# Forget-gate layer: values and decays computed among the input projections, 128 tokens per score tile, one carried state, norm by pairs of heads

## The reference, cut to what matters

```
proj = h @ w_in                                   # q_pre, f_pre, i_val, g_out, 1024 columns each
f = lb + (1 - lb) * sigmoid(f_pre);  k = 1 - f;  q = silu(q_pre)
b = cumsum(log f, inside a chunk);  b_ref = b[C/2 - 1];  b_last = b[C - 1]
scores = (q * exp(b - b_ref)) @ (k * exp(b_ref - b)).T, causal, inside a chunk
o_intra = scores @ v
q_dec = q * exp(b);  k_dec = k * exp(b_last - b)
for each chunk:  o_inter = q_dec @ S;  S = exp(b_last) * S + k_dec.T @ v
o = o_intra + o_inter
o = o * rsqrt(mean(o^2 over the head) + eps) * norm_g * silu(g_out)
y = o @ w_out
```

## Time and profile before

| | us |
|---|---|
| median of 3 runs | 2901.13 |
| range | 2897.42 to 2907.69 |
| the profiled execution | 2895.93 |
| its span | 2893.8 |
| TensorE busy | 2489.5 |
| VectorE busy | 2036.6 |
| ScalarE busy | 1397.0 |

### The profile page before, as it was taken

The page is one execution under the profiler, slowest core; times in us unless marked ns, Lnnn a source line. Parts: engine busy times, 40 slices in busy tenths (PEclk is TensorE's granted clock), DMA queues, the critical chain, the costliest instruction groups (busy, mean ns, idle before and its releaser), DMA issues. The chain is left out here.

```text
span 2893.8 us, 46933 instructions
## 1 busy us (share of the span) xinstructions
PE 2489.5 (86%) x18972; PEld 2361.8 (82%) x18972; DVE 2036.6 (70%) x3448; ACT 1397.0 (48%) x2474; POOL 92.4 (3%) x85
## 2 busy tenths in 40 slices
PE   3888999988789998859999569997777999976998
PEld 3677999967789998749999469997557999865997
DVE  3476788645767875978877638886247788757885
ACT  4543565356155644436635316745314575433673
POOL 0010000000100000800000000000000000000000
PEclk8799999988899999979999759999978999988999
DMA  4022667722045776214567204573104556641452
GB/s 183 31 86 74 233 220 290 302 91 88 15 169 196 263 286 235 90 37 157 199 263 277 73 2 160 194 289 115 59 0 175 206 194 245 243 175 38 153 195 96
DMA packets 63367, 462.91 MB, mean 160 GB/s; under 512 B 7024, under 2 KB 7088, under 8 KB 7216
## 3 DMA queue, kind: packets, MB, share of 16 engines
q1 hardware_dynamic: 62640, 456.16, 42.6%
q10 hardware_dynamic: 512, 3.77, 0.3%
HBM read 458.85 MB, written 1.05 MB: 159 GB/s over the span
## 5 line engine op out<-in xcount | busy, mean ns | idle before, releaser
L727 PE MATMUL psum<-arena_rounded,upper_rounded 128*128 128x256 f32 (+1 forms) x5208 | 1477.8, 284 | 149.6 <-PEq L629 55.2
L728 PE MATMUL psum<-arena_rounded,upper_rounded 128*128 128x256 f32 (+1 forms) x5208 | 1464.7, 281 | 0.0
L729 PE MATMUL psum<-arena_rounded,ring_rounded 128*128 128x256 f32 (+1 forms) x5208 | 1464.5, 281 | 0.0
L727 PEld LDWEIGHTS psum<-arena_rounded,upper_rounded 128*128 128x128 f32 (+1 forms) x5208 | 992.4, 191 | 167.6 <-issue 87.6
L544 DVE TENSOR_TENSOR ring_rounded<-ring,upper_rounded 128x1024 fp32r<-128x1024 f32 (+4 forms) x990 | 847.2, 876 | 336.3 <-ACT upper_rounded L535 331.5
L535 ACT ACTIVATE upper_rounded<-ring 128x1024 fp32r<-128x1024 f32 (+4 forms) x990 | 758.1, 775 | 636.3 <-PE psum L729 543.9
L728 PEld LDWEIGHTS psum<-arena_rounded,upper_rounded 128*128 128x128 f32 (+1 forms) x5208 | 997.0, 191 | 1.5 <-issue 1.4
L729 PEld LDWEIGHTS psum<-arena_rounded,ring_rounded 128*128 128x128 f32 (+1 forms) x5208 | 995.0, 191 | 0.1
L566 DVE SCALAR_TENSOR_TENSOR ada_sum<-ring,small,ada_sum 128x1024 f32<-128x1024 f32 x168 | 214.7, 1278 | 1.0
L2372 DVE SCALAR_TENSOR_TENSOR arena<-psum,cols,arena 128x255 f32<-128x255 f32 (+1 forms) x352 | 153.2, 477 | 55.5 <-ACT arena L2339 52.4
L2339 ACT ACTIVATE arena<-psum,cols 128x256 f32<-128x256 f32 x176 | 89.4, 561 | 44.2 <-PE psum L729 44.2
(11 more groups left out here) (460 smaller groups left out, 2551.3 us busy)
## 6 DMA issues: line engine op xcount, KB each, us to landing
ring<-stream_dram SPq DMA_DIRECT2D x434, 1024.0 KB, 4.9
const<-const_dram ACTq DMA_DIRECT2D x1, 1607.0 KB, 7.1
x<-x_dram ACTq DMA_DIRECT2D x1, 1024.0 KB, 9.1
out_dram<-x SPq DMA_DIRECT2D x1, 1024.0 KB, 3.9
cols<-cols_dram ACTq DMA_DIRECT2D x1, 982.0 KB, 10.6
...
```

Source lines behind the costliest of these rows:

```text
L727: pe.matmul(out, upper, x[0][:, b.k, :], start=(b.k == 0), stop=False)
L728: pe.matmul(out, upper, x[1][:, b.k, :], start=False, stop=False)
L729: ins = pe.matmul(out, lower, x[0][:, b.k, :], start=False, stop=(b.k == nk - 1))
```

## The change

`hgrn_in` now opens with the feed-forward block before it and holds four projections in the order f, values, q, g, each of f and q with one side number. GpSimd writes the scan's restart marks. ScalarE takes the logarithm of f during the values, VectorE scans and subtracts during q, ScalarE takes the exponentials during g, by halves of four heads, and VectorE multiplies. The gate keeps its raw value until the next block.

`hgrn` is one block. The 256 tokens are two tiles of 128. Inside each tile, scores inside a chunk are as before (16 matmuls); scores beyond a chunk are 48 matmuls of a chunk's 32 decayed keys with all later queries of the tile, which have been multiplied by the decays of the chunks between. Both land in one 128 x 128 score tile. Only one state per head is left, that after the first 128 tokens, from 8 transposes and 8 matmuls. The output takes 3 matmuls per head. Norm, gate and split go by pairs of heads. The diff, cut (removed code is in the kernel above):

```diff
-            g["hg_qfg", i] = with_sides(by_rounds(matrix("hg_w_in_2", (0,), D, tiles(0, 2 * KD))
-                                                  + matrix("hg_w_in_2", (0,), D, tiles(3 * D, KD)), TOGETHER), sides(2))
+            part = lambda n: matrix("hg_w_in_2", (0,), D, tiles(n * D, KD))
+            g["hg_f", i] = with_sides(by_rounds(part(1), TOGETHER), sides(1))
             g["hg_v", i] = by_rounds(matrix("hg_w_in_2", (0,), D, tiles(2 * D, 2, BANK)))
+            g["hg_q", i] = with_sides(by_rounds(part(0)), sides(1))
...
+    return [slot2(chip, n) for n in (1, 2, 3, 5, 6, 7, 8, 9, 10)]
...
+    @block.gpsimd
+    def _(pool):
+        pool.memset(t2, 1.0).then_inc(restart_ready, 1)
+        pool.wait_ge(restart_ready, 1)
+        pool.memset(chunks(t2)[:, :, 0:1], 0.0).then_inc(restart_ready, 1)
+
+    def forget(block, s, banks, steps):
...
+            for c in range(steps):
+                s["act_step"](act, c)
+                act.wait_ge(s["ready"], s["through"](c))
+                if c >= 2:
+                    act.wait_ge(forgets_ready, c - 1)
+                act.activation(e[c % 2], banks(c)[0], ACT.Sigmoid).then_inc(s["free"], 1)
+            w.act(act, s["last"])
...
+            for c in range(steps):
+                s["dve_step"](dve, c)
+                dve.wait_ge(s["free"], c + 1)
+                dve.tensor_scalar(f[:, c, :], e[c % 2], chip.lb_rest[:, c:c + 1], chip.lb[:, c:c + 1],
+                                  ALU.mult, ALU.add).then_inc(forgets_ready, 1)
+                if c:
+                    dve.wait_ge(forgets_ready, c)
+                    dve.tensor_scalar(k[:, c - 1, :], f[:, c - 1, :], -1.0, 1.0, ALU.mult, ALU.add)
+            dve.wait_ge(forgets_ready, KD)
...
+    @block.tensor
+    def _(pe):
+        for at, b in enumerate(blocks):
+            n = at // KD
+            if at == KD:
+                pe.wait_ge(fs["free"], 6)
+            if at == 0 or blocks[at - 1].chunk is not b.chunk:
+                pe.wait_ge(w.lower_ready, b.chunk.order + 1)
+            upper, lower = w.parts(b)
+            for tt in range(NT):
+                bank, sl = chip.bank(v_bank(n, tt), b.width), slice(tt * P, (tt + 1) * P)
+                pe.matmul(bank, h[0][:, b.k, sl], upper, start=(b.k == 0), stop=False)
+                pe.matmul(bank, h[0][:, b.k, sl], lower, start=False, stop=False)
+                ins = pe.matmul(bank, h[1][:, b.k, sl], upper, start=False, stop=(b.k == KD - 1))
+            if b is b.chunk.end:
+                ins.then_inc(w.used, 1)
+
...
+        for n in range(2):
+            act.wait_ge(forgets_ready, KD)
+            act.activation(f[:, halves[n], :], f[:, halves[n], :], ACT.Ln).then_inc(logs_ready, 1)
+            w.act(act, ends[n] - 1)
+            act.wait_ge(w.used, ends[n] + 1)
+            act.activation(v[:, 0, n * BANK:(n + 1) * BANK], chip.bank(v_bank(n, 0)), ACT.Identity).then_inc(v_ready, 1)
+        w.act(act, ends[1])
+
+    @block.vector
+    def _(dve):
+        for n in range(2):
+            w.dve(dve, ends[n] - 1)
+            dve.wait_ge(w.used, ends[n] + 1)
+            dve.tensor_copy(v[:, 1, n * BANK:(n + 1) * BANK], chip.bank(v_bank(n, 1))).then_inc(v_ready, 1)
+        w.dve(dve, ends[1])
...
+            for c in range(steps):
+                s["dve_step"](dve, c)
+                if c == 0:
+                    dve.wait_ge(restart_ready, 2)
+                    dve.wait_ge(fs["dve_done"], 1)
+                part = halves[c // 4]
+                at = lambda n: chunks(b_sum[:, part, :])[:, :, n:n + 1].broadcast_to([P, KD // 2 * (T // C_HG), C_HG])
+                if c % 4 == 0:
+                    dve.wait_ge(logs_ready, c // 4 + 1)
+                    chain(dve.tensor_tensor_scan(flat(b_sum[:, part, :]), flat(t2[:, part, :]), flat(f[:, part, :]), 0.0,
+                                                 ALU.mult, ALU.add))
+                if c % 4 == 1:
+                    dve.tensor_tensor(chunks(t1[:, part, :]), chunks(b_sum[:, part, :]), at(C_HG // 2 - 1),
+                                      ALU.subtract).then_inc(exponents_ready, 1)
+                if c % 4 == 2:
+                    dve.tensor_tensor(chunks(t2[:, part, :]), at(C_HG - 1), chunks(b_sum[:, part, :]),
+                                      ALU.subtract).then_inc(exponents_ready, 1)
...
+    def after_values(pe, step):
+        if step < 2:
+            pe.wait_ge(v_ready, 4)
+        else:
+            pe.wait_ge(fs["free"], 5 + step)
+
+    qs = project(chip, st, ("hg_q", i), KD, queries, x=h, entry=after_values)
...
+            for c in range(steps):
+                s["act_step"](act, c)
+                part = halves[c // 4]
+                act.wait_ge(exponents_ready, 2 * (c // 4) + 2)
+                to, src, sign = ((f, b_sum, 1.0), (ke, t1, -1.0), (qe, t1, 1.0), (t2, t2, 1.0))[c % 4]
+                act.activation(to[:, part, :], src[:, part, :], ACT.Exp, scale=sign).then_inc(exps_ready, 1)
+                if c == 4:
+                    act.activation(decay, chunks(b_sum)[:, :, C_HG - 1], ACT.Exp)
+                act.wait_ge(s["ready"], s["through"](c))
+                act.activation(g[:, c, :], banks(c)[0], ACT.Identity).then_inc(s["free"], 1)
...
+            dve.wait_ge(qs["free"], KD)
+            for c in range(steps):
+                s["dve_step"](dve, c)
+                part = halves[c // 4]
+                dve.wait_ge(exps_ready, c + 1)
+                to, other = ((f, q), (ke, k), (qe, q), (k, t2))[c % 4]
+                if c % 4 == 3:
+                    dve.wait_ge(multiplied, c // 4 + 1)
+                ins = dve.tensor_tensor(to[:, part, :], to[:, part, :], other[:, part, :], ALU.mult)
+                if c % 4 == 1:
+                    ins.then_inc(multiplied, 1)
...
+    def after_queries(pe, step):
+        pe.wait_ge(qs["free"], 5 + step)
+
+    project(chip, st, ("hg_g", i), KD, outputs, x=h, entry=after_queries)
...
+            for n in range(2):
+                for j in range(both[n].start, both[n].stop):
+                    ins = pe.matmul(diagonal(n)[:, j - both[n].start, :], tiles_of(ke)[:, j, :], tiles_of(qe)[:, j, :],
+                                    start=True, stop=True)
+                ins.then_inc(diagonal_ready, 1)
+            pe.wait_ge(copied, 1)
+            pe.wait_ge(later_ready, 1)
+            for n in range(2):
+                for j in range(both[n].start, both[n].stop):
+                    keys = lambda m: tiles_of(kd)[:, j, m * C_HG:(m + 1) * C_HG]
+                    to = lambda m: beyond(n)[m * C_HG:(m + 1) * C_HG, j - both[n].start, (m + 1) * C_HG:P]
+                    pe.matmul(to(0), keys(0), later0[:, j, :], start=True, stop=True)
+                    pe.matmul(to(1), keys(1), later1[:, j, :], start=True, stop=True)
+                    ins = pe.matmul(to(2), keys(2), tiles_of(qd)[:, j, 3 * C_HG:P], start=True, stop=True)
+                ins.then_inc(beyond_ready, 1)
+            pe.wait_ge(last_ready, 2)
+            pe.wait_ge(clamped, 1)
...
+                ins = pe.transpose(turned[:, hd, :], k_last[:, hd, :], chip.con("ident"))
             ins.then_inc(turned_ready, 1)
-
-        @block.vector
-        def _(dve):
-            dve.wait_ge(scores_ready, 1)
-
-            Chain(dve, dve_chain)(dve.tensor_scalar(scores, ps, BIG, -BIG, ALU.min, ALU.max))
-            dve.tensor_tensor(scores, scores, over(chip.con("chunk"), 2 * H_HG), ALU.mult)
-
-        @block.scalar
+            pe.wait_ge(turned_copied, 1)
+            pe.wait_ge(clamped, 2)
+            for hd in range(H_HG):
+                ins = pe.matmul(state_ps[:, hd, :], k_tok[:, hd, :], v[:, 0, hd * P:(hd + 1) * P], start=True, stop=True)
+                if hd % 4 == 3:
+                    ins.then_inc(state_ready, 1)
+            pe.wait_ge(inter_ready, 2)
+            for n, pair in enumerate(pairs):
+                pe.wait_ge(scores_ready, n // 2 + 1)
+                pe.wait_ge(state_copied, n // 2 + 1)
+                for hd in range(pair.start, pair.stop):
+                    out = chip.bank(4 + n, T, at=(hd - pair.start) * T)
+                    vh = slice(hd * P, (hd + 1) * P)
+                    pe.matmul(out[:, 0:P], v[:, 0, vh], scores[:, hd * NT, :], start=True, stop=True)
+                    pe.matmul(out[:, P:T], v[:, 1, vh], scores[:, hd * NT + 1, :], start=True, stop=False)
+                    ins = pe.matmul(out[:, P:T], state[:, hd, :], q_inter[:, hd, :], start=False, stop=True)
+                ins.then_inc(o_ready, 1)
+            for n, pair in enumerate(pairs):
+                pe.wait_ge(squared, n + 1)
+                pe.matmul(chip.bank(n), chip.con("ones"), flat(squares[:, pair, :]), start=True,
+                          stop=True).then_inc(var_ready, 1)
+
...
+            act.activation(later0[:, :, 0:C_HG], part(1), ACT.Identity)
+            act.activation(later1[:, :, 0:C_HG], part(2), ACT.Identity).then_inc(copied, 1)
```

(68 more changed lines are left out.)

212 lines of the change are left out of this document (83 added, 129 removed).

## The result

The changed kernel takes 2829.03 us (median of 4 runs, 2824.97 to 2830.21); the kernel before took 2899.28 beside it, a ratio of 0.9756 with a 95% interval from 0.9726 to 0.9786. The prediction was 2835. The kernel before has its median here over 4 runs; the 2901.13 ahead of the prediction was over 3 of them. The profiled execution took 2828.80 us with a span of 2827.0, against 2895.93 and 2893.8 before: 66.8 us of span.

What follows compares the result with a forecast made beforehand. TensorE's projection stream bounds it, except the serial recurrence chain. Front 1616.5 + 2.5 + 3.2 = 1622.2, plus 40, starts the output projection at 1662.2, not 1727.9: 65.7 us less, 2835.4 on the median; predicted 2835, range 2826 to 2850.

Steps and rivals of the forecast that it cites:

- Projections, value blocks: Front: q, f, g projections take 71.7 us as before, values 22.0; the border, over 2 us idle, goes.
- Starving: In q, TensorE waits for weight splits queued behind VectorE's added work: about 2.5 us, bounds 0 and 6.7.
- The value copies' wait: Ahead of q, whose first two tiles reuse the values' banks: one 512-wide copy and its handover, 0.9 us.
- The tail of g: From TensorE's last g matmul to the recurrence: split, eighth exponential, multiplication, stage border, 3.2 us (bounds 1.5 and 3.5).
- Clock over the scores: Recurrence's first score matmuls: after about 3 us idle, half clock takes 6.8 us instead of 3.4, +3.4.
- Rival B: Half clock through the whole recurrence, since a busy TensorE alone does not restore it: +10 us, 2846; chance 0.22.
- Scores beyond a chunk: Recurrence: 48 new matmuls with 32-column weights take 6.2 us, ends 3 and 9.6; 2.6 if column groups run concurrently.
- The walk behind them: Rest of the recurrence at full clock: last output pair at 21.2, sums 24.6, first root 27.2, end 35.7 us.
- The clock allowance: Recurrence: 36 us with the clock full throughout, about 50 at half clock, best 35; 40 taken.
- Rival D: Whole change cheaper: clock full, column groups concurrent, nothing starves, recurrence 35 us: 2826 us; chance 0.08.
- C: Starved projections: VectorE in f and q, ScalarE in g; 6.7 and some 3 us show: 2843 to 2845; chance 0.12.
- Its signs: Last g matmul near 1619, scores 3 us later, small matmuls 5 to 7 us, recurrence 40, low clock over scores.

Runs made afterwards that it cites:

- The wider spread: Changed kernel with the modulation pieces on the f and q projections spread over 15 blocks each instead of 10: 2823.10 us, ratio 0.9734.

## Why the prediction was right

The main mechanism was right: the decays went under the projections, and the chained states went from the path. The total came out 6 us below the forecast and inside its range, but terms were off in opposite directions, and how near it came is luck. For the profiled execution the working gave 2830.2, and it took 2828.80, only 1.4 us less. By the prediction's own steps, from the first forget-gate matmul:

| step | predicted | measured |
|---|---|---|
| front, without tail | 97.1 | 101.1 |
| tail from g to the recurrence | 3.2 | 1.9 |
| recurrence to output projection | 40 | 31.3 |
| to the output projection in all | 140.3 | 134.4 |

**Projections, value blocks.** Right: the values took 22.4 us (22.0), and the border between q, f, g and the values went. The 0.118 us for each matmul was the kernel before's; 199 of the changed kernel's came at 0.113.

**Starving.** The size was right and the place was wrong. I put 2.5 us of waiting into q, for weight splits. There is none worth naming in q and g; TensorE waited 2.04 us in f instead, and there it was ScalarE, held up by a weight transfer.

**The value copies' wait.** This term was mis-sized: 0.9 predicted, 3.4 measured. I had priced one copy and its handover and not what stands ahead of it on VectorE: two modulation pieces of 1.33 us each. Behind it the clock fell as well, another 1.5 us, and a fall of the clock inside q was one of the prediction's own signs of being wrong. It had no term for it. The wider spread gave back 1.4 us of the wait and all of the clock's part.

**The tail of g.** 1.9 against 3.2, inside the bounds: the last matmul at 1622.18, the last exponential until 1622.73, the last multiplication until 1623.99. My chain had a split of 1.06 us ahead of the exponential on the path; it was one of 0.63, and had ended before TensorE's last matmul. The terms of that chain also add up to 3.4 us, not to the 3.2 written.

**Clock over the scores.** Half right. The forecast took +3.4 us for half clock. In the changed kernel the scores ran at 1.00 (3.81 us for 32 records) after an idle time of 1.9 us; in four of the kernels above, after 1.9 or 2.5 us, they took 5.44 us. So the mechanism exists, at half the price, and only in some executions. Rival B, half clock through the recurrence, is out: no run with the new recurrence showed it, while the old recurrence behind the new front had a mean of 0.59.

**Scores beyond a chunk.** The largest error among the steps of the walk: 6.2 predicted, 2.8 measured, 4.5 if ordered against the overlap. The lower end of my own range was right. The Trainium skill (TensorE: Matmul & The Clock Gate, "Part 3: Packing small matmuls") lets tiles in different column groups run together; by that rule the prediction had 2.6 us, and the traces of both orders bear it out (2.8 and 4.5 us). That the switch between tilings drains the array (the Trainium skill, TensorEngine Tiling (Array Packing), "Key Properties") shows no cost that can be read here: the small matmuls begin at 1628.10, with the scores' last ending at 1628.17, and 32 groups of three records, 0.083 us apart, fill all but 0.1 us of the 2.8 up to the transposes.

**The walk behind them.** Counting from the first score: updates from 9.2 us, the last output matmul at 16.7, the sums done at 20.3, VectorE's first scaling, right behind the first root, at 23.2, output projection at 31.3. Predicted were 21.2, 24.6, 27.2 and 35.7 for the last four. The whole gain against that walk, 4.5 us, was made up to the last output matmul; behind the last output matmul it had 14.5 us and the trace has 14.7. The clock allowance of 4 us on top was not used; with the 4.5 us it makes the 8.7.

**The sum.** Front 2.7 us too small, recurrence 8.7 too large, start and output projection 1.7 us shorter, and 6.5 us more behind the block, which no step had and which the change does not cause: 2.7 - 8.7 - 1.7 + 6.5 = -1.2 (the last 0.2 of the 1.4 are rounding and the time outside the span). Without the 6.5 us the forecast for the profiled execution would have been 8 us too high. Rival D (cheaper) came true in the recurrence, and went further than its 35 us. The front without its tail was 4 us dearer than the forecast, but not by C's mechanism: neither splits in q nor exponentials in g held TensorE up. No case of the list was the right one.

**Its signs.** Of what would show the forecast, the short tail behind g came (1.9 us), and the two prices that would have refuted it did not: the small matmuls took 0.06 us each, not over 0.2, and the norm's tail 14.7 us, under 15. But TensorE's last g matmul was at 1622.2 and not near 1619, a gap of 2.0 us stood in f, the small matmuls took 2.8 us and not 5 to 7, the recurrence 31.3 and not 40, and the lower clock lay over q and not over the scores. The number stood; much of the path to it did not. A misreading without weight: the outputs of before are 16 long matmuls with the short ones between them, not 24 blocks.
